# Two more seven-product groups per quarter of an MLP, with a new order of products, folds and splits

## The reference, cut to what matters

```python
h2 = rms_norm(x, norm_ffn_g[l])                              # x: 256 tokens x 2048
u = jnp.square(jax.nn.relu(jnp.einsum('bsd,df->bsf', h2, w_up[l])))   # 2048 x 8192
x = x + jnp.einsum('bsf,fd->bsd', u, w_down[l])              # 8192 x 2048
return rms_norm(x, norm_final_g)
```

## Time and profile before

| | |
|---|---|
| runs | 1480.06, 1480.27, 1481.33 us; median 1480.27 |
| the profiled execution | 1481.53 us |
| its span, first to last instruction | 1479.7 us |
| PE busy | 1466.2 us (99%) |
| DVE / ACT busy | 1103.8 us (75%) / 767.0 us (52%) |
| granted clock, mean | 0.999 of 2.4 GHz |
| DMA | 316 MB, 214 GB/s over the span |

### The profile page before, as it was taken

The page is one execution under the profiler, slowest core; times in us unless marked ns, Lnnn a source line. Parts: engine busy times, 40 slices in busy tenths (PEclk is TensorE's granted clock), DMA queues, the critical chain, the costliest instruction groups (busy, mean ns, idle before and its releaser), DMA issues.

```text
span 1479.7 us, 18698 instructions
## 1 busy us (share of the span) xinstructions
PE 1466.2 (99%) x6968; PEld 1278.7 (86%) x6968; DVE 1103.8 (75%) x1366; ACT 767.0 (52%) x986; POOL 15.0 (1%) x21
## 2 busy tenths in 40 slices
PE   9999999999999999999999999999999999999997
PEld 7888888888888888888888888888888888888876
DVE  7977887776577788777799756885588657785667
ACT  7656565444455555444454555555554555455553
POOL 0100000000000000000000000000000000000000
PEclk9999999999999999999999999999999999999999
DMA  9556544667656565556765787658766787668843
GB/s 324 195 170 209 187 155 163 228 204 245 211 173 194 176 198 190 186 193 213 246 221 198 249 255 236 207 193 276 258 204 207 246 257 228 218 216 248 259 166 142
DMA packets 161320, 316.11 MB, mean 214 GB/s; under 512 B 6512, under 2 KB 14832, under 8 KB 161008
## 3 DMA queue, kind: packets, MB, share of 16 engines
q1 hardware_dynamic: 149168, 297.51, 60.4%
q10 hardware_dynamic: 12096, 17.84, 4.1%
HBM read 304.84 MB, written 10.49 MB: 213 GB/s over the span
## 4 chain that ended last, share of the span: by engine, by line
PE 96%; DVE 2%; DMA 1%; issue 1%; ACT 0%; SPq 0%; POOLq 0%; POOL 0%; DVEq 0%
PE acc L618 86%; PE acc L908 3%; PE banks L855 3%; PE acc L855 1%; DVE wlo L1386 1%; PE banks L637 1%; PE banks L656 1%; PE banks L646 0%; DMA raw<-in_w_down 0%; DMA raw<-in_w_in 0%; DVE ta_lo L1986 0%; PE banks L753 0%; DVE sum_lo L1976 0%; PE banks L769 0%; PE banks L768 0%
## 5 line engine op out<-in xcount | busy, mean ns | idle before, releaser
L946 ACT ACTIVATE whi<-raw 128x1024 fp32r<-128x1024 f32 x542 | 568.9, 1056 | 601.9 <-PE acc L618 532.5
L1386 DVE TENSOR_TENSOR wlo<-raw,whi 128x1024 fp32r<-128x1024 f32 x542 | 656.5, 1222 | 298.9 <-ACT whi L946 295.2
L618 PE MATMUL acc<-whi,ta_hi 128*128 128x512 f32 x1308 | 497.4, 380 | 0.6 <-DVE wlo L1475 0.6
L618 PE MATMUL acc<-wlo,ta_hi 128*128 128x512 f32 x1308 | 495.7, 379 | 0.0
L618 PE MATMUL acc<-whi,ta_lo 128*128 128x512 f32 x1308 | 495.7, 379 | 0.0
L618 PEld LDWEIGHTS acc<-whi,ta_hi 128*128 128x128 f32 x1308 | 247.2, 189 | 37.6 <-issue 2.1
L618 PEld LDWEIGHTS acc<-whi,ta_lo 128*128 128x128 f32 x1308 | 247.2, 189 | 35.1
L618 PEld LDWEIGHTS acc<-wlo,ta_hi 128*128 128x128 f32 x1308 | 247.3, 189 | 34.4
L618 PE MATMUL acc<-whi,tb_hi 128*128 128x512 f32 x560 | 212.7, 380 | 2.7 <-DVE wlo L1386 2.7
L618 PE MATMUL acc<-wlo,tb_hi 128*128 128x512 f32 x560 | 212.2, 379 | 0.0
L618 PE MATMUL acc<-whi,tb_lo 128*128 128x512 f32 x560 | 212.2, 379 | 0.0
(11 more groups left out here) (213 smaller groups left out, 1070.5 us busy)
## 6 DMA issues: line engine op xcount, KB each, us to landing
raw<-in_w_in SPq DMA_DIRECT2D x64, 1024.0 KB, 5.2
raw<-in_w_up SPq DMA_DIRECT2D x64, 1024.0 KB, 5.3
raw<-in_w_down SPq DMA_DIRECT2D x57, 1024.0 KB, 5.0
raw<-in_w_gate SPq DMA_DIRECT2D x32, 1024.0 KB, 5.4
raw<-in_w_att SPq DMA_DIRECT2D x16, 1024.0 KB, 5.0
raw<-in_w_ret SPq DMA_DIRECT2D x16, 1024.0 KB, 5.0
raw<-in_w_out SPq DMA_DIRECT2D x16, 1024.0 KB, 5.1
parking<-buf ACTq DMA_DIRECT2D x16, 512.0 KB, 3.9
```

Of the source, the lines that this page charges most:

```text
L618: last = nc.tensor.matmul(paired(acc[B.parity][:, t, :]), a[:, k, tok], halves_in_turn(b), start=(k == 0 and n == 0), stop=(k == (B.ends + ...
L946: nc.scalar.activation(whi[:, B.ring_at(u), :], raw[:, B.raw_at(u), :], ACT.Copy).then_inc(hi_ready, 1)
L1386: V_.tensor_tensor(wlo[:, at, :], raw[:, B.raw_at(u), :], whi[:, at, :].bitcast(f32), ALU.subtract).then_inc(lo_ready, 1)
```

## The change

`LATE` gets two more entries, so that up blocks 0, 2 and 3 each host a group (c = 3 for j, k = 0, 1; c = 2 for 0, 1; c = 2 for 2, 3). 6 groups more run (9 late, 4 boundary). The down blocks of the first three quarters have 4 units each, and the order for `wide` false, which stood unused, is taken there. Chunk 2 has to be fetched and mixed again in the next quarter: 4 DMAs on ACT's queue at its start, `mixed_tokens`, `mixed_hi_of` and `mixed_lo_of` in up block 1. In the groups PE's order becomes: the two plain corner products, S1T1, S2T2, S4, S3T3, the last corner product, which for late groups now has a bank of its own (`fourth`, one fold more). DVE's folds, splits and low halves follow other orders, and in the last quarter the adds of D0 and D1 stand behind more splits.

```diff
-BOUNDARY_FOLDS, LATE_FOLDS = 5, 7
+BOUNDARY_FOLDS, LATE_FOLDS = 5, 8
-LATE = {0:(0,1,3)}
+LATE = {0:(0,1,3),2:(0,1,2),3:(2,3,2)}
...
# PE, seven_products
                 pe.wait_ge(mixed_lo_ready, G.mixed)
-                pe.wait_ge(sum_lo_ready, G.halves(2))
-                pe.wait_ge(folded, G.folds(1))
-                product(chain, S2, T2, stop=True).then_inc(product_done, 1)
+                pe.wait_ge(sum_lo_ready, G.halves(1))
...
                 product(right, S1, T1, start=True, stop=True).then_inc(product_done, 1)
+                pe.wait_ge(sum_lo_ready, G.halves(2))
+                pe.wait_ge(folded, G.folds(1))
+                product(chain, S2, T2, stop=True).then_inc(product_done, 1)
+                pe.wait_ge(lo_ready, E.low(u + 2))
+                pe.wait_ge(folded, G.folds(2))
+                product(right, S4, weights(u + 2), stop=not G.standing).then_inc(unit_done, 1)
                 pe.wait_ge(sum_lo_ready, G.halves(3))
-                pe.wait_ge(folded, G.folds(2))
+                pe.wait_ge(folded, G.folds(3))
                 product(chain, S3, T3, stop=True).then_inc(product_done, 1)
...
-                    pe.wait_ge(folded, G.folds(4))
-                    product(chain, units(lower, 1), weights(u + 3), stop=True).then_inc(unit_done, 1)
+                    product(fourth, units(lower, 1), weights(u + 3), start=True, stop=True).then_inc(unit_done, 1)
# ACT, stage6, the down phase
-                    split(Q.down[1], 1, 2)
+                    split(Q.down[1], 1, 3)
...
-                    split(Q.down[1], 2, 4)
-                    split(Q.J, 0, 1)
+                    split(Q.down[1], 3, 4)
+                    split(Q.J, 0, 2)
                     hi_from_exchanged(Q.turn(q, 4), 3)
-                    split(Q.J, 1, 2)
                     mixed_hi_of(GROUPS - 1, q * MIXES_OF_QUARTER)
+                done = 0 if wide else 2
                 if last:
+                    split(Q.J, 0, 2)
                     residual_squares(Q.down_end[0], 0, down_sq, buf[1])
-                done = 0 if wide else 2
+                    done = 2
# DVE, stage6, the down phase
                 if not wide:
-                    split(Q.J, 0, 1)
+                    split(Q.J, 0, 2)
                 mixed_tokens(Q.turn(q, 4), q * MIXES_OF_QUARTER)
                 lo_from_exchanged(q * 4 + 16, 3)
...
                 mixed_lo_of(GROUPS - 1, q * MIXES_OF_QUARTER)
...
                 if last:
                     split(Q.down_end[0], 6, 8)
-                    split(Q.down_end[1], 6, 7)
+                    split(Q.down_end[1], 6, 8)
+                    split(Q.J, 0, 1)
                     add_residual(Q.down_end[0], 0)
-                    split(Q.down_end[1], 7, 8)
+                    split(Q.J, 1, ready)
...
                 add_residual(Q.down_end[1], 1)
# DVE, sums_for_seven (after T3)
-                sums_lo(G, 0)
+                split(E, u - 1, u)
                 dve.wait_ge(sum_set, G.sums(3))
                 V_.tensor_tensor(right_up, T2, left_low, ALU.add).then_inc(sum_set, 1)
-                split(E, u - 1, u)
-                sums_lo(G, 1)
                 split(E, u, u + 2)
-                sums_lo(G, 2)
+                for m in range(SUMS):
+                    sums_lo(G, m)
# DVE, fold_to_bank; fold_in_passing opens in the same way
-                split(E, u + 2, u + 3)
                 dve.wait_ge(unit_done, E.unit(u))
                 fold(0, G.j, chain, ALU.add)
+                split(E, u + 2, u + 3)
+                dve.wait_ge(product_done, G.products(1))
+                fold(1, G.k, acc[K.parity][:, 0, :], ALU.add)
                 split(E, u + 3, u + 4)
-                dve.wait_ge(product_done, G.products(1))
+                dve.wait_ge(product_done, G.products(2))
                 fold(0, G.k, chain, ALU.subtract)
-                dve.wait_ge(product_done, G.products(2))
-                fold(1, G.k, acc[K.parity][:, 0, :], ALU.add)
                 part(K, 0, 1)
                 dve.wait_ge(product_done, G.products(3))
```

More of the change, by code:

```diff
@@ L340, in build @@
         chain, second, third = rs_ps[1], rs_ps[0], banks[:, 0, 0].rearrange(flat)
+        fourth = banks[:, 0, 1].rearrange(flat)
         raw_full = [sem(f"raw_full{s}") for s in range(LOADS)]
@@ L1333, in split_for_seven @@
                 sums_hi(G, 1, 2)
-                split(B, u - 1, u)
+                split(B, u - 1, u + 1)
                 sums_hi(G, 2, 3)
-                split(B, u, u + 3)
+                split(B, u + 1, u + 3)
                 act.wait_ge(sum_set, G.sums(SUMS + 1))
@@ L1843, in stage6 @@
                 if not wide:
-                    split(Q.J, 0, 1)
+                    split(Q.J, 0, 2)
                 mixed_tokens(Q.turn(q, 4), q * MIXES_OF_QUARTER)
                 lo_from_exchanged(q * 4 + 16, 3)
+                done = 0 if wide else 2
+                ready = min(3, Q.boundary.at - 2) if Q.boundary else 3
                 if wide:
@@ L1849, in stage6 @@
                 else:
-                    split(Q.J, 1, 2)
+                    split(Q.J, done, ready)
                 mixed_lo_of(GROUPS - 1, q * MIXES_OF_QUARTER)
@@ L1855, in stage6 @@
                     split(Q.down_end[0], 6, 8)
[L1856 removed]
+                    split(Q.down_end[1], 6, 8)
+                    split(Q.J, 0, 1)
                     add_residual(Q.down_end[0], 0)
[L1858 removed]
+                    split(Q.J, 1, ready)
+                elif wide:
+                    split(Q.J, done, ready)
                 G = Q.boundary
[L1860 to L1862 removed]
                 add_residual(Q.down_end[1], 1)
@@ L1911, in sums_for_seven, with first_folds @@
                 V_.tensor_tensor(T3, right_up, right_low, ALU.add).then_inc(sum_set, 1)
-                sums_lo(G, 0)
+                split(E, u - 1, u)
                 dve.wait_ge(sum_set, G.sums(3))
                 V_.tensor_tensor(right_up, T2, left_low, ALU.add).then_inc(sum_set, 1)
-                split(E, u - 1, u)
-                sums_lo(G, 1)
                 split(E, u, u + 2)
-                sums_lo(G, 2)
+                for m in range(SUMS):
+                    sums_lo(G, m)
+            def first_folds(G):
+                E, u = G.entries, G.at
+                dve.wait_ge(unit_done, E.unit(u))
+                fold(0, G.j, chain, ALU.add)
+                split(E, u + 2, u + 3)
             def fold_to_bank(G, K, part):
                 E, u = G.entries, G.at
-                split(E, u + 2, u + 3)
-                dve.wait_ge(unit_done, E.unit(u))
-                fold(0, G.j, chain, ALU.add)
+                first_folds(G)
+                dve.wait_ge(product_done, G.products(1))
+                fold(1, G.k, acc[K.parity][:, 0, :], ALU.add)
                 split(E, u + 3, u + 4)
-                dve.wait_ge(product_done, G.products(1))
+                dve.wait_ge(product_done, G.products(2))
                 fold(0, G.k, chain, ALU.subtract)
-                dve.wait_ge(product_done, G.products(2))
-                fold(1, G.k, acc[K.parity][:, 0, :], ALU.add)
                 part(K, 0, 1)
                 dve.wait_ge(product_done, G.products(3))
-                dve.wait_ge(folded, G.folds(3))
+                dve.wait_ge(folded, G.folds(2))
                 fold(1, G.k, chain, ALU.subtract)
@@ L1943, in fold_in_passing @@
                 E, u = G.entries, G.at
-                split(E, u + 2, u + 3)
-                dve.wait_ge(unit_done, E.unit(u))
-                fold(0, G.j, chain, ALU.add)
+                first_folds(G)
+                dve.wait_ge(product_done, G.products(1))
+                fold(1, G.k, third, ALU.add)
                 split(E, u + 3, u + 4)
-                dve.wait_ge(product_done, G.products(1))
+                dve.wait_ge(product_done, G.products(2))
                 fold(0, G.k, chain, ALU.subtract)
-                dve.wait_ge(product_done, G.products(2))
-                fold(1, G.k, third, ALU.add)
-                dve.wait_ge(product_done, G.products(3))
                 dve.wait_ge(folded, G.folds(3))
-                fold(1, G.k, chain, ALU.subtract)
+                fold(0, G.j, second, ALU.add)
                 split(B, 6, 7)
-                fold(0, G.j, second, ALU.add)
                 dve.wait_ge(unit_done, E.unit(u + 2))
                 fold(0, G.k, third, ALU.add)
+                dve.wait_ge(product_done, G.products(3))
+                fold(1, G.k, chain, ALU.subtract)
+                fold(1, G.j, chain, ALU.add)
+                split(B, 7, 8)
                 dve.wait_ge(unit_done, E.unit(u + 3))
-                fold(1, G.j, chain, ALU.add)
+                dve.wait_ge(folded, G.folds(7))
+                fold(1, G.j, fourth, ALU.add)
             def mixed_tokens(turn, before):
```

4 lines of the change are left out of this document (removed).

## The result

The changed kernel takes 1487.46 us (median of five runs, 1486.94 to 1489.31), the kernel before 1480.27: a ratio of 1.005, 95% interval 1.0039 to 1.0061. It is slower. The forecast was 1478.9, with an upper end of 1483.2, so the time lies outside the range, on the side that had a chance of 0.14. The profiled execution took 1486.94 us, its span is 1485.1, that is 5.4 more than before.

The account below looks back on a forecast made before the run. PE, nearly gapless, was taken as the bound: -7.77 - 3.47 + 2.16 + 0.3 + 7.4 = -1.4 us on the profiled 1481.53 gave 1480.1, less 1.26 to the median 1478.9 us. Range 1475.0 to 1483.2.

Parts of the forecast that it names:

- Costed at nothing: Step pricing the second mixing, its DMAs, ACT's high halves and SP's loads at zero, as covered by other work.
- products, 36 matmuls: Each of 6 new groups does seven products for eight on PE: -7.77 us, all on the path.
- last quarter's end, loss: Reordered splits and adds cut PE's waits at the last quarter's end to 1.4 us from 4.87: -3.47 us.
- J's third unit, each of three: Short down phase, first three quarters: PE waits for DVE's late split, 0.87 us each with the restart.
- boundary group, each of three: Group after the short down phase: DVE's first fold comes 1.35 us too late, 1.60 us lost each.
- sixth product, block 0, each: Up block 0's late group: PE waits for DVE's third fold, 0.24 us with the restart.
- late group of block 2, each: Up block 2: the new order's wait for the third fold, 0.24 us; DVE in time by 0.1 us.
- late group of block 3, each: Up block 3: the third-fold wait, 0.24 us, plus 0.1 for the corner loads' landing.
- the last line of the sum: Took the profiled run's surplus of 1.26 us over the median off 1480.1, giving 1478.9.
- The waits: Rivals: the predicted DVE waits partly or all stay away, 1476.5, 1475.2 or about 1468; chance 0.30 together.
- The corners: Rival: corner loads land late in up block 3, about 6.4 us in all three quarters, 1483.3; chance 0.12.
- The short waits: Rival: many short waits drop PE to 1.2 GHz in three boundary groups, 1506; chance 0.02 with unseen causes.

Follow-up runs that it names:

- loop written out: PE's loop over quarters 1 and 2 unrolled, other engines keeping theirs: 1481.77 us in the changed kernel, 1479.28 in the kernel before.
- Shifted by 64: 64 more PE instructions (repeated waits on a semaphore already there) ahead of PE's loop: 1480.09 us in the changed kernel, 1484.06 in the kernel before.
- shifted by 76: The kernel before with 76 more PE instructions (repeated waits) ahead of PE's loop: 1479.38 us.
- by 32: The kernel before with 32 more PE instructions (repeated waits) ahead of PE's loop: 1481.23 us.
- by 224: The changed kernel with 224 more PE instructions (repeated waits) ahead of PE's loop: 1480.88 us.
- the adds alone: The kernel before with only the last quarter's part: DVE's splits ahead of its add, two ACT splits ahead of the squares, old product order: 1476.46 us.
- one added host: The changed kernel with two late hosts (up blocks 0 and 2) in place of three, and PE's loop unrolled: 1476.35 us.
- old order, three hosts: The kernel before, its product order, last quarter's adds moved, up blocks 2 and 3 added as late hosts, PE's loop unrolled: 1501.34 us.
- shifted by 240: The changed kernel with 240 more PE instructions (repeated waits) ahead of PE's loop: 1485.86 us.
- early fold: The changed kernel with DVE's third fold put ahead of the fourth corner's split in all 13 groups: 1488.86 us.

## Why the prediction was wrong

**The step that failed** is the one headed "Costed at nothing". It went through DVE, ACT, the DMA queues and SP for work without cover, and left out PE's own program. The change takes 96 matmuls out ahead of PE's loop, the loop slides to a packet's end, its code is fetched again for the second pass, and its branch back costs 6.66 us in the profiled run. None of my rivals had this place. The Trainium skill, Runtime: NRT & Kernel Launch, section Instruction fetch mechanics, says that a taken branch whose target is no longer held forces a fetch before execution can go on; it also gives the program's blocks as 16 KiB, and the 16.4 KB of the q8 line agree. It names a window of two pages for this, but gives PE 128 KiB, that is eight such blocks. Here a loop over seven packets was kept, and one over eight was not.

**The other terms**, by the changed kernel's profiled run (predicted, then measured, us):

| term | predicted | measured |
|---|---|---|
| products, 36 matmuls | -7.77 | -7.77 |
| last quarter's end, loss | 1.4 | 1.38 |
| J's third unit, each of three | 0.87 | 0.86, 0.79, 0.79 |
| boundary group, each of three | 1.60 | 1.53, 1.46, 1.47 |
| sixth product, block 0, each | 0.24 | 0.18, 0.18, 0.24 |
| late group of block 2, each | 0.24 | 0.20, 1.03, 0.25 |
| late group of block 3, each | 0.34 | 0.54, 0.55, 0.25 |
| branch back of the loop | none | 6.66 |

With the 4.87 lost before, -7.77 - 4.87 + 1.38 + 6.90 + 3.42 = -0.94 without the branch, where I had -1.4; with it +5.72, and the spans differ by 5.4. The 1.03 in block 2 is of quarter 2, the first behind the branch; with the loop written out it is 0.26, so it is an effect of the gap. Shifted by 64, without a gap, the last quarter's end, J with the boundary groups, and the late groups lose about 1.4, 7.0 and 2.8 us: -1.4, as forecast, and that span is 2.0 below before's.

**A second, smaller fault** is in the last line of the sum: I took the profiled run's surplus of 1.26 over the median off the forecast. But that surplus very likely sat in the very waits that the change removes: the other profiled runs of before's list lose 3.2 (loop written out), 3.1 (shifted by 76), 3.0 (by 64) and 4.1 us (by 32) at the last quarter's end, not 4.87, and the two of them that lose nothing at the branch, written out and shifted by 76, take 1479.14 and 1479.35. The sum should have been set against 1481.53 alone, which gives 1480.1. Where its loop's code was not fetched again, the changed kernel took 1480.09 (shifted by 64), 1480.88 (by 224) and 1481.77 (written out): 1.2 to 2.9 us above the forecast of 1478.9, and at most 1.7 above 1480.1.

**The rivals.** The waits did appear, near their size. The corners did not land late: in up block 3, the rival's place, T1 waited about 0.25 us for the turn in quarters 1 and 2, and 0.18 for the landing in the last quarter; at that quarter's end the landing held T1 by 0.16 us, not 3.61. The short waits did not lower the clock: shifted by 64 the kernel has all of them, and a granted clock of 0.999. What the Trainium skill, TensorE: Matmul & The Clock Gate, section A second HAM failure mode: psum-queue depth-cycling, tells of another kernel, a clock that swings with frequent micro-idles, no run here shows. In the changed kernel the clock did fall, but in and behind the gaps at the branch.

**What the change is worth by its parts.** The last quarter's moved adds give 4.4 us by themselves (1480.85 less 1476.46). The two added hosts and the new order take most of them away again even without the branch: the waits, 6.90 + 3.42 + 1.38 = 11.70 us, or 10.93 without the 0.77 that the gap added in block 2, are 3.2 more than the products' 7.77. The medians say the same: 1480.09 shifted by 64, against 1476.46 with the adds alone. With one added host the products' 3.89 are about what the waits cost (PE loses 4.0 us there, 0.3 with the adds alone), and the time is that of the moved adds.

## What to carry to other kernels

Before a change to a hand-written instruction list is costed, count what it adds or removes ahead of each loop, and look at the instruction queues' packets during the loop's second pass: a loop that is held now can cost several microseconds at its branch after an edit that never touches it, and a written-out loop or a few idle instructions give them back. Look at the times of all executions as well: where the loop's code was fetched again, one kernel's executions lay up to 6 us apart, and a trace shows one of them. When the profiled run is slower than the median, find where, and do not subtract the surplus if the change removes that place. An experiment that changes one part alone would have shown here that one small reordering carries all the gain.

## What I had not expected of the hardware

- A loop of some 750 matmuls on PE ran its second pass without a single packet of its program being fetched, and 64 idle instructions ahead of it decided that, both ways: -7.4 us in the changed kernel (1487.46 to 1480.09), +3.1 in the kernel before (1480.98 to 1484.06).
- Idle instructions cost nothing themselves: 224 of them (448 repeated waits) between the products of quarter 0 left PE without a further gap there.
- A long gap need not lower the clock. It was at 1.00 behind 2.54 us (old order, three hosts) and 2.83 us (shifted by 240, the profiled execution), and fell behind 2.27 us (early fold, a wait at J's third unit in quarter 2) and within 2.96 us (the changed kernel). What decides it these runs do not show.
